# A hybrid encoder layer on one core: x transposed unscaled, 1/rms applied as projections leave PSUM

## What is computed

```python
def rmsnorm(x, gain):
    y = x * lax.rsqrt(jnp.mean(x * x, axis=-1, keepdims=True) + EPS)
    return y * gain

h = rmsnorm(x, norm_gain)
proj = h @ w_in                      # 4096 x 20480 columns
qa, ka, va, za, qb, fb, ib, zb, ga, gb = split(proj)
a = window_sink_attention(qa, ka, va, sinks) * silu(za)      # 16 heads of 128, 4 kv heads
ob = hgrn2_chunkwise(qb, fb, ib, lower_bound(lb_logits))     # 16 heads, sigmoid(f), silu(q)
b = rms_per_head(ob) * hgrn_gain * silu(zb)
y = sigmoid(ga) * (a @ w_up_attn) + sigmoid(gb) * (b @ w_up_hgrn)
out = rmsnorm(x + y @ w_out, final_norm_gain)
```

## Time and profile before

| what | value |
|---|---|
| median of three runs | 2718.64 us |
| the profiled execution, its own time | 2718.89 us |
| its span | 2717.1 us |
| mean granted TensorE clock | 0.998 |
| PE, DVE, ACT busy | 98%, 59%, 53% of the span |
| moved by DMA | 503.06 MB, mean 185 GB/s |

### The profile page before, as it was taken

How to read it: one execution, slowest core, us unless ns; L and a number is a source line. 1 busy time by engine, 2 the same in 40 slices (tenths; PEclk the granted TensorE clock), 3 DMA queues, 4 the chain that set the end, 5 groups by cost and what they waited for, 6 DMA issues and landing times.

```text
span 2717.1 us, 39928 instructions
## 1 busy us (share of the span) xinstructions
PE 2672.5 (98%) x12249; PEld 2219.6 (82%) x12249; DVE 1614.5 (59%) x3055; ACT 1447.8 (53%) x2373; POOL 0.2 (0%) x4
## 2 busy tenths in 40 slices
PE   7999999999999999999999999999999999999997
PEld 5888888888878888888888888888888888888886
DVE  6557777777777775555555555555555555655554
ACT  5546556566555565555554444444444444554544
POOL 0000000000000000000000000000000000000000
PEclk9999999999999999999999999999999999999999
DMA  6666555565555565656666666666666666666665
GB/s 207 191 189 176 163 169 172 161 174 174 157 175 164 164 178 172 182 171 178 174 192 193 193 188 193 191 191 193 192 191 190 193 189 194 201 217 205 214 212 184
DMA packets 258546, 503.06 MB, mean 185 GB/s; under 512 B 15568, under 2 KB 15776, under 8 KB 258080
## 3 DMA queue, kind: packets, MB, share of 16 engines
q1 hardware_dynamic: 258464, 502.05, 61.7%
HBM read 497.80 MB, written 4.19 MB: 185 GB/s over the span
## 4 chain that ended last, share of the span: by engine, by line
PE 95%; DVE 2%; issue 1%; ACT 1%; DMA 0%; SPq 0%; ACTq 0%; DVEq 0%
PE acc L393 30%; PE acc L395 30%; PE acc L394 30%; PE lev L413 1%; DVE w_lo L842 1%; DVE lev_m L913 1%; PE acc L405 1%; DVE at_m L920 1%; PE lev L415 0%; DMA sink<-in_attn_sinks_dram 0%; PE lev L543 0%; ACT sq_x L674 0%; PE mis L441 0%; PE mis L426 0%; PE lev L450 0%
## 5 line engine op out<-in xcount | busy, mean ns | idle before, releaser
L842 DVE TENSOR_TENSOR w_lo<-raw,w_hi 128x512 fp32r<-128x512 f32 x1856 | 1262.2, 689 | 917.5 <-ACT w_hi L592 917.1
L592 ACT ACTIVATE w_hi<-raw 128x512 fp32r<-128x512 f32 x1856 | 1148.6, 629 | 1040.0 <-PE acc L395 1033.1
L393 PE MATMUL acc<-w_hi,h_hi 128*128 128x512 f32 x3200 | 1267.2, 396 | 7.2 <-DVE w_lo L842 6.6
L394 PE MATMUL acc<-w_hi,h_lo 128*128 128x512 f32 x3200 | 1246.7, 390 | 2.1 <-issue 2.1
L395 PE MATMUL acc<-w_lo,h_hi 128*128 128x512 f32 x3200 | 1248.0, 390 | 0.0
L393 PEld LDWEIGHTS acc<-w_hi,h_hi 128*128 128x128 f32 x3200 | 601.5, 188 | 136.1 <-DVE w_lo L842 14.8
L395 PEld LDWEIGHTS acc<-w_lo,h_hi 128*128 128x128 f32 x3200 | 601.0, 188 | 129.6 <-issue 2.3
L394 PEld LDWEIGHTS acc<-w_hi,h_lo 128*128 128x128 f32 x3200 | 601.7, 188 | 120.7
L393 PE MATMUL acc<-w_hi,a_hi 128*128 128x512 f32 x256 | 99.6, 389 | 0.0
L394 PE MATMUL acc<-w_hi,a_lo 128*128 128x512 f32 x256 | 99.6, 389 | 0.0
L395 PE MATMUL acc<-w_lo,a_hi 128*128 128x512 f32 x256 | 99.6, 389 | 0.0
(11 more groups left out here) (162 smaller groups left out, 1066.0 us busy)
## 6 DMA issues: line engine op xcount, KB each, us to landing
raw<-in_w_in_dram SPq DMA_DIRECT2D x672, 512.0 KB, 3.6
raw<-in_w_out_dram SPq DMA_DIRECT2D x128, 512.0 KB, 3.7
raw<-in_w_up_attn_dram SPq DMA_DIRECT2D x64, 512.0 KB, 3.6
raw<-in_w_up_hgrn_dram SPq DMA_DIRECT2D x64, 512.0 KB, 3.6
xr<-in_x_dram SPq DMA_DIRECT2D x8, 512.0 KB, 4.5
x_in<-in_x_dram SPq DMA_DIRECT2D x3, 1024.0 KB, 8.1
out_dram<-xr SPq DMA_DIRECT2D x6, 512.0 KB, 4.8
fgain<-in_final_norm_gain_dram SPq DMA_DIRECT2D x8, 256.0 KB, 5.9
```

Source lines behind the costliest of these rows:

```text
L393: nc.tensor.matmul(o, l_hi[:, kt, tok], w_hi[:, s, :], start=kt == 0, stop=False)
L394: nc.tensor.matmul(o, l_lo[:, kt, tok], w_hi[:, s, :], start=False, stop=False)
L592: nc.scalar.activation(w_hi[:, k % RING, :], raw[:, (k // 2) % RING, k % 2, :], ACT.Copy).then_inc(hi_ready, 1)
L842: nc.vector.tensor_tensor(w_lo[:, k % RING, :], raw[:, (k // 2) % RING, k % 2, :], w_hi[:, k % RING, :].bitcast(F32), ALU.subtract).then_i ...
```

## The change

The pieces of x are cut by columns for both token tiles at once, and issued one ahead of each of the first four weight transfers. norm_gain and the identity are issued first by SP, and ACT issues the other vectors and the sinks itself. x is transposed as it lands, and h_hi and h_lo hold x times gain. The squares of 512 columns each are taken in the first block after steps 4, 7, ... 25: ACT those of token tile 0, DVE those of tile 1. Sum, root and reciprocal follow at steps 28, 30 and 31. Every eviction of a w_in block becomes two ACTIVATEs, one for each token tile, whose scale is the token's 1/rms. PE's own instructions are the same ones. The core of the diff:

```diff
+X_CUTS = [0, 512, 1536, 2560, D]
+SQ = 512
+SQ_N = D // SQ
+SQ_AT = [4 + 3 * i for i in range(SQ_N)]
...
+            sp.dma_start(vrow[0:32, :], norm_gain...).then_inc(vec_in, 16)
+            sp.dma_start(tab[:, T_ID:], tables[:, T_ID:]).then_inc(ident_in, 16)
+            def load_x(i):
+                cols = slice(X_CUTS[i], X_CUTS[i + 1])
+                sp.dma_start(x_in[:, :, cols], x_rows[:, :, cols]).then_inc(x_landed[i], 16)
             def load_first(w, col):
                 for r in range(RING):
+                    load_x(r)
                     sp.dma_start(raw[:, r, :, :], w[:, 2 * r:2 * r + 2, bass.ds(col, BLK)]).then_inc(w_landed[r], 16)
...
             def input_pair(p):            # PE
-                pe.wait_ge(x_scaled, p + 1)
-                if p < 3:
-                    pe.wait_ge(x_scaled_1, p + 1)
+                pe.wait_ge(x_landed[x_piece(2 * p * P)], 16)
...
+            def scaled(rows_sb, par, func):    # ACT
+                for t in range(TT):
+                    m = nc.scalar.activation(rows_sb[:, t, :], acc[:, par, t * BLK:(t + 1) * BLK], func, scale=small[:, 8 + t:9 + t])
+                return m
             def stage(rows_sb, par, n_end, func):
                 act.wait_ge(pe_done, n_end)
-                nc.scalar.activation(rows_sb[:, :, :], acc[:, par, :]..., func).then_inc(staged, 1)
+                scaled(rows_sb, par, func).then_inc(staged, 1)
...
-            act.wait_ge(sink_in, 16)
+            act.dma_start(vrow[32:64, :], lb_logits...).then_inc(vec_in, 16)
+            act.dma_start(vrow[64:80, :], hgrn_norm_gain...).then_inc(vec_in, 16)
+            act.dma_start(sink[:, :], attn_sinks...).then_inc(sink_in, 16)
...
+            input_pair(0)                 # ACT; DVE likewise
             round_step(count(0), 0, fresh=True)
             round_step(count(0), 1, fresh=True)
-            input_pair(0)
...
+                            if k in SQ_AT:          # ACT; DVE likewise for tile 1
+                                x_squares(SQ_AT.index(k))
+                            if k == KT - 2:
+                                act.wait_ge(xs_sum, TT)
+                                nc.scalar.activation(small[:, 6:8], small[:, 4:6], ACT.Sqrt, scale=1.0 / D, bias=eps_t[:, :]
+                                                     ).then_inc(xs_root, 1)
...
+                            if k == KT - 4:         # DVE
+                                dve.wait_ge(xsq, SQ_N)
+                                dve.wait_ge(xsq_v, SQ_N)
+                                for t in range(TT):
+                                    nc.vector.tensor_reduce(small[:, 4 + t:5 + t], sums[:, t, :], AX_X, ALU.add).then_inc(xs_sum, 1)
+                            if k == KT - 1:
+                                dve.wait_ge(xs_root, 1)
+                                nc.vector.reciprocal(small[:, 8:10], small[:, 6:8]).then_inc(xs_rs, 1)
...
-            for p in range(3):
-                scale_pair(p)
```

More of the change, by code:

```diff
@@ L82 @@
 T_ALL = T_MEAN + P
-X_PIECES = [(0, 0, D // 2, D // 2), (0, D // 2, D, 3 * D // 4),
-            (1, 0, D // 2, D // 2), (1, D // 2, 3 * D // 4, 3 * D // 4), (1, 3 * D // 4, D, 7 * D // 8)]
+X_CUTS = [0, 512, 1536, 2560, D]
+SQ = 512
+SQ_N = D // SQ
+SQ_AT = [4 + 3 * i for i in range(SQ_N)]
 FINAL = [0, BLK] + [D - BLK - i * 2 * BLK for i in (2, 1, 0)] + [D]
@@ L145, in build @@
         small = sb("small", [P, 16])
-        sums = sb("sums", [P, 2 * len(X_PIECES)])
+        sums = sb("sums", [P, TT, SQ_N])
         eps_t = sb("eps_t", [P, 1])
@@ L185, in build @@
         proj, _ = at(proj_base, "proj", [P, NB, GH * SEQ])
-        sq_x, q = at(proj_base, "sq_x", [P, D // 2])
-        sq_v, q = at(q, "sq_v", [P, D // 4])
+        sq_x, q = at(proj_base, "sq_x", [P, SQ])
+        sq_v, q = at(q, "sq_v", [P, SQ])
         q = proj_base + 4 * 4 * GH * SEQ
@@ L201, in build @@
         assert q <= proj_base + 4 * NB * GH * SEQ
-        sig_b = k_att
+        sig_b = k_att[:, :, :].rearrange("p h t -> p (h t)").rearrange("p (t n) -> p t n", t=TT)
         y_row = v_att
@@ L217, in build @@
         ident_in, tab_in, vec_in, sink_in = sem("ident_in"), sem("tab_in"), sem("vec_in"), sem("sink_in")
-        x_landed = [sem(f"x_landed{i}") for i in range(len(X_PIECES))]
+        x_landed = [sem(f"x_landed{i}") for i in range(len(X_CUTS) - 1)]
         eps_set = sem("eps_set")
-        xsq, xsq_v, sums_zero = sem("xsq"), sem("xsq_v"), sem("sums_zero")
-        xs_sum, xs_root, xs_rs, x_scaled, x_scaled_1 = sem("xs_sum"), sem("xs_root"), sem("xs_rs"), sem("x_scaled"), sem("x_scaled_1")
+        xsq, xsq_v = sem("xsq"), sem("xsq_v")
+        xs_sum, xs_root, xs_rs = sem("xs_sum"), sem("xs_root"), sem("xs_rs")
         x_tr, h_hi_done, h_lo_done = sem("x_tr"), sem("h_hi_done"), sem("h_lo_done")
@@ L289, in hinted, with x_piece @@
             return nc.Fori(1, end, engines=(engine.engine,), hint_back_edge=True)
+        def x_piece(col):
+            return next(i for i in range(len(X_CUTS) - 1) if X_CUTS[i] <= col < X_CUTS[i + 1])
         block = ctx.enter_context(nc.Block())
@@ L295, in _ @@
         def _(sp):
[L296 to L303, removed]
+            sp.dma_start(vrow[0:32, :], norm_gain.rearrange("a (c p) -> (a c) p", p=P)).then_inc(vec_in, 16)
+            sp.dma_start(tab[:, T_ID:], tables[:, T_ID:]).then_inc(ident_in, 16)
+            def load_x(i):
+                cols = slice(X_CUTS[i], X_CUTS[i + 1])
+                sp.dma_start(x_in[:, :, cols], x_rows[:, :, cols]).then_inc(x_landed[i], 16)
             def load_steps(n, w, col, steps, first=0):
@@ L592, in round_step @@
                 nc.scalar.activation(w_hi[:, k % RING, :], raw[:, (k // 2) % RING, k % 2, :], ACT.Copy).then_inc(hi_ready, 1)
+            def scaled(rows_sb, par, func):
+                for t in range(TT):
+                    m = nc.scalar.activation(rows_sb[:, t, :], acc[:, par, t * BLK:(t + 1) * BLK], func, scale=small[:, 8 + t:9 + t])
+                return m
             def stage(rows_sb, par, n_end, func):
                 act.wait_ge(pe_done, n_end)
-                nc.scalar.activation(rows_sb[:, :, :], acc[:, par, :].rearrange("p (t n) -> p t n", t=TT), func).then_inc(staged, 1)
+                scaled(rows_sb, par, func).then_inc(staged, 1)
             def hgrn_epilogue(b, par, n_end, slot):
@@ L602, in hgrn_epilogue @@
                     act.wait_ge(pe_done, n_end)
-                    nc.scalar.activation(flat(slot + 2), acc[:, par, :], ACT.Copy).then_inc(i_copied, 1)
+                    scaled(rows(slot + 2), par, ACT.Copy).then_inc(i_copied, 1)
                 else:
@@ L663, in attn_load, with x_squares @@
                     nc.scalar.activation(vw[:, :, :], v_att[:, :, bass.ds(g * HD, HD)], ACT.Copy).then_inc(qvw_done, 1)
-            act.wait_ge(sink_in, 16)
+            act.dma_start(vrow[32:64, :], lb_logits.rearrange("a (c p) -> (a c) p", p=P)).then_inc(vec_in, 16)
+            act.dma_start(vrow[64:80, :], hgrn_norm_gain.rearrange("a (c p) -> (a c) p", p=P)).then_inc(vec_in, 16)
+            act.dma_start(sink[:, :], attn_sinks.broadcast_to([P, HEADS])).then_inc(sink_in, 16)
             act.wait_ge(eps_set, 1)
             nc.scalar.activation(small[:, 0:1], eps_t[:, :], ACT.Sqrt)
-            for i, (t, first, end, cut) in enumerate(X_PIECES):
-                act.wait_ge(x_landed[i], 16)
+            def x_squares(i):
+                act.wait_ge(x_landed[x_piece(i * SQ)], 16)
                 if i:
                     act.wait_ge(xsq, i)
-                nc.scalar.activation(sq_x[:, 0:cut - first], x_in[:, t, first:cut], ACT.Square, accum_out=sums[:, i:i + 1]
+                nc.scalar.activation(sq_x[:, :], x_in[:, 0, i * SQ:(i + 1) * SQ], ACT.Square, accum_out=sums[:, 0, i:i + 1]
                                      ).then_inc(xsq, 1)
-            act.wait_ge(xs_sum, TT)
-            nc.scalar.activation(small[:, 6:8], small[:, 4:6], ACT.Sqrt, scale=1.0 / D, bias=eps_t[:, :]).then_inc(xs_root, 1)
-            act.wait_ge(xs_rs, 1)
-            for p in range(3):
-                cols = slice(2 * p * P, 2 * (p + 1) * P)
-                nc.scalar.activation(x_in[:, 1, cols], x_in[:, 1, cols], ACT.Copy, scale=small[:, 9:10]).then_inc(x_scaled_1, 1)
             act.wait_ge(vec_ready, 1)
@@ L709, in hgrn_group @@
                         if first and b == 1 and k == 4:
+                            act.wait_ge(sink_in, 16)
+                            act.wait_ge(xs_rs, 1)
                             act.wait_ge(lb_chain, 2)
@@ L736, in _ @@
                             act.wait_ge(pe_done, n(2 * KT))
-                            nc.scalar.activation(v_att[:, :, :], acc[:, 1, :].rearrange("p (t c) -> p t c", t=TT), ACT.Copy).then_inc(kv_copied, 1)
+                            scaled(v_att, 1, ACT.Copy).then_inc(kv_copied, 1)
                         else:
@@ L790, in merge @@
                         act.wait_ge(pe_done, n(KT))
```

(25 more changed lines are left out.)

## The result

Measured: 2707.95 us, median of six runs (2707.25 to 2709.28), beside 2718.45 before (six runs, 2716.52 to 2720.26). That is 10.5 us less, a ratio of 0.9962 (95% interval 0.9949 to 0.9975). The profiled execution took 2707.25 us with a span of 2704.7, 12.4 us under the span before. It is the fastest of its six, so the median's 10.5 is the better figure for the gain.

What follows compares the result with a forecast made beforehand. TensorE was taken as the bound from step 0 on, so only a shorter start could gain: 2718.89 - 12.58 = 2706.3 us profiled, 2706.1 on the median's scale, other terms at no change; range 2703 to 2709.

Steps and rivals of the forecast that it cites:

- (a): Start: squares, root, scaling and sinks wait leave the path; step 0 at about 10.9 instead of 23.48, gain 12.6 us.
- the hole of small transfers: DMA stream from 7 to 10 us, 218 GB/s where small transfers stand; taken as no loss, other end 1.5 us.
- The other path, by the vectors: Second way to step 0, through x piece 0 and the vectors: 10.0, or 12.6 if the vectors land late.
- (b): Stream after step 0: fourth weights land at 20.4, step 6 may start at 21.9, PE comes at 22.8; nothing lost.
- this floor: Weight landings limit step 6, so a step 0 earlier than 10.0 would buy nothing.
- (c): First block: eight squares per engine hide beside PE; cost 0, at most 8 x 0.3 us if the ring ran dry.
- (d): 42 evictions become two ACTIVATEs each, +0.3 us apiece, hidden by the ring; cost 0, other end 6.3 us.
- The cover: Behind the costliest eviction, from the next w_lo's end (224.54) to PE's use (225.57): 1.03 us, need 0.3.
- (e): After step 0: slow matmul pace costs the same 2.3 us as before; ends 2.3 better or 1.4 worse.
- R1: Rival: the stream or the vectors bind, step 0 at 13 to 14.5, time 2708.4 to 2710; chance 0.17.

Runs made afterwards that it cites:

- the second profile of the changed kernel: The changed kernel run once more, unchanged, as the measure for three kernels built on it: 2708.23 us.
- the extra transposes: 12 and 10 transposes of the identity around the first two pairs, keeping PE at work before step 0, against the changed kernel with the sinks' transfer last: 2710.36 us.
- another order: Against the changed kernel with the sinks' transfer last: pair 2 transposed after step 0, x pieces 2 and 3 after the third and fourth weight transfer; 2705.51 us.
- the sinks last: Changed kernel with the sinks' transfer issued by SP behind the first sixteen weight transfers, not by ACT at the start: 2706.22 us.
- the sinks twice: Changed kernel with the sinks' transfer made twice at the start, the second copy into its own tile: 2708.55 us.

## Why the prediction was right, step by step

**(a) The way to step 0: the mechanism holds, the size was 1.8 us too large.** Step 0 was to start at 10.9 and started at 12.70. The 12.58 us of the forecast are 10.78. The term that was mis-sized is the landing of x piece 1, forecast at 9.8, measured 11.90. The working carried the stream's rate from the earlier trace rows over and took the hole of small transfers at no loss. The hole came along, from 7 to 10 us down to 3 to 6 us, and there it lies ahead of piece 1. Without the sinks' packets the piece lands at 10.33 and step 0 starts at 11.13; the second profile of the changed kernel has 11.26 and 12.07, so the hole's price there is 0.9 us and here 1.6. The end that was given for this, 1.5 us of stream, is about what was lost. The hole had been named, and the wrong one of its two ends taken. It is not all: even without the sinks' packets the piece lands 0.5 us later than the working had it, which stays open, and from landing to step 0 it took 0.8 us where 1.05 were put.

The other path, by the vectors, was as assumed: vec's transpose starts at 3.6, and the small transfers landed 1.6 to 2.3 us after their issue, nearer the 3.1 than the 6.9 of the earlier trace rows. ACT issued the two that vec needs at 0.74 and 1.20, ahead of x's first piece (1.66) and not at 2.0 as the working had it, so they did not have to wait among x's packets. The sinks, issued at 1.67, did wait, and landed at 7.5; on ACT's queue they took the stream's time all the same. The Trainium skill (DMA: Bandwidth & Descriptors, Issuing engines are not separate DMA queues) says that transfers of different issuers interleave on the same DMA engines. The trace agrees: the sinks' 128 packets ran from 3.7 to 7.0 us between those of x.

**(b) The stream after step 0 keeps up: right, barely.** w_hi waited four times for weights, 6.9 us in all, and PE not once before step 8. The fourth transfer was there at 22.3 against the 20.4 forecast, most of it by the same hole (20.7 without the sinks' packets). The w_lo of step 6 was done 0.4 us before PE came to it, where 0.9 had been forecast. That an earlier step 0 would run into this floor was right too: with the extra transposes and the same order of transfers, PE waited until 21.99, and only another order moved it.

**(c) The squares in the first block: cost 0, right.** Seven of eight left out saved nothing of the first block's 51.5 us.

**(d) The evictions: cost 0, right.** One of 512 columns took 0.685 and the pair 1.27 against 1.03 before; 0.3 us was forecast, 0.24 measured. Timelines of ACT, DVE and PE, answering to the earlier trace rows:

```profile
211.00 1.27 ACT L601 ACTIVATE turn_h<-acc,small 128x512 f32<-128x512 f32 x2
```

```profile
212.82 0.69 DVE L856 TENSOR_TENSOR w_lo<-raw,w_hi 128x512 fp32r<-128x512 f32 x1 [0.45 <-ACT w_hi L596]
```

```profile
214.29 0.39 PE L399 MATMUL acc<-w_hi,h_hi 128*128 128x512 f32 x1
```

The cover shrank from 1.03 to 0.78 us and was not used up. The waits for a w_lo are 21 times and 6.4 us, and the split alone, in the kernel before, cost nothing.

**(e) The clock: the same slow pace was forecast, and it came out a little shorter, which is chance.** It was over 3.7 us after step 0 (12.70 to 16.4) against 4.9 before, which gave 0.5 us by step 32. In the second profile of the changed kernel it gave 0.1. It also varies without any change to the start: the kernel before with its evictions in two had the fast pace from 23.02, 0.3 us after its step 0, so the 2.3 us of the working are no fixed price. Another 1.3 us of the profiled span lie in one stop of PE near 800 us, 2.1 us long before and 0.8 after. It varies from profile to profile (0.8 and 1.6 in two of the changed kernel, 2.2 in that with the evictions in two), so it belongs to the spread and not to the change.

The sum: 10.78 for step 0, 0.5 for the pace and 1.3 for the stop, less 0.2 elsewhere, give the 12.4 of the profiled spans. That they come so near to the 12.58 of the forecast is luck: step 0 gave 1.8 less, and the pace and the stop gave it back. The better measure is the medians' 10.5, near the 10.78 of step 0, the one term that the change owns. The forecast of 2706.1 was 1.9 too low and inside its range. Of the rivals R1 had named the mechanism behind most of it, the hole, and priced it too high: step 0 at 13 to 14.5 and 2708.4 to 2710, against 12.70 and 2707.95.

## What to carry to other kernels

When work leaves the head of a kernel, the first transfers become the path, and each small one ahead of or beside them must be priced in stream time and not in bytes: here 8 KB in 64-byte packets cost 0.9 to 1.6 us, and a second such transfer beside the first hardly more. A scale that commutes with a matmul can be applied at the eviction for nothing, where a ring of staged operands covers the longer eviction; read the cover as the distance from the last staged operand to its use. A faster start needs its data in the order in which the steps use them, or the gain turns into a wait further on.

## What the runs showed of the hardware

The broadcast of 16 floats to 128 partitions, 128 packets of 64 bytes, held the stream at 136 GB/s for 3 us where 296 were moved without it, though issued on the other engine's queue.

TensorE's granted clock read 1.00 in the slices at the start, where matmuls stood 0.43 apart (the 1.2 GHz level). That 1.00 is no measurement: the trace's records of the clock begin with its first rise (at 28.09 us in the kernel before, at 16.24 in the changed one), and a stretch without a record reads as full. Later slow stretches have records and did show, with 0.93 over 575 to 600 us. After stops of 1.84, 2.38 and 2.52 us matmuls came back at the slow pace; after one of 2.1 us near 800 us the kernel before did not. The plainest pair is that of the sinks last and the sinks twice: at the end of the loop both stop for 2.03 us, the first has matmuls 0.43 apart from 1.5 us after it on, the second stays at 0.23. So the length of the stop does not tell.

In all three kernels with twenty or twenty-two transposes more in PE's program, PE stops at both edges between passes of the HGRN loop (1.2 to 1.6 us near 395, 1.8 to 2.5 near 597) and not at the loop's end. In the eleven without them it stops at the loop's end (0.8 to 2.2 us near 800) and not at the edges. What moves the stops was not tested, and their cause stays open.
